# A two-block transformer kernel: the FFN's gate and up products by five Strassen groups, its second product by one

## The reference

```python
def swiglu(h, w_gate, w_up, w_down):            # D_MODEL 1024, D_FF 2816 = 22 chunks of 128
    return (jax.nn.silu(h @ w_gate) * (h @ w_up)) @ w_down

x = x + rms_norm(m, g_post_mix)                 # m: attention @ w_o
h = rms_norm(x, g_pre_ffn)
x = x + rms_norm(swiglu(h, w_gate, w_up, w_down), g_post_ffn)
```

## Time and profile before

| | before |
|---|---|
| median of 3 runs | 1280.83 us |
| profiled execution, its own time | 1281.71 us |
| its span | 1279.6 us |
| PE busy | 1270.1 us, 99% |
| DVE busy | 761.4 us, 60% |
| ACT busy | 594.1 us, 46% |
| DMA, moved | 181.01 MB |

### The profile page before, as it was taken

How to read it: one execution, slowest core, us unless ns; L and a number is a source line. 1 busy time by engine, 2 the same in 40 slices (tenths; PEclk the granted TensorE clock), 3 DMA queues, 4 the chain that set the end, 5 groups by cost and what they waited for, 6 DMA issues and landing times.

```text
span 1279.6 us, 16976 instructions
## 1 busy us (share of the span) xinstructions
PE 1270.1 (99%) x6329; PEld 1061.1 (83%) x6329; DVE 761.4 (60%) x1554; ACT 594.1 (46%) x1239; POOL 49.9 (4%) x97
## 2 busy tenths in 40 slices
PE   9999999999999999999999999999999999999998
PEld 8887777898888888888888888788878788999987
DVE  4366776654555455547675678675545534976664
ACT  5366676543453345335453324563335542463533
POOL 1010100100000000000100010000000000000000
PEclk9999999999999999999999999999999999999999
DMA  6279894222252236232525898212221022353531
GB/s 249 99 214 257 241 263 141 70 99 99 99 198 99 99 122 222 85 132 99 171 94 173 243 273 238 77 67 99 99 99 67 33 99 100 125 195 125 197 133 66
DMA packets 31937, 181.01 MB, mean 141 GB/s; under 512 B 3944, under 2 KB 4204, under 8 KB 12784
## 3 DMA queue, kind: packets, MB, share of 16 engines
q1 hardware_dynamic: 24360, 141.19, 31.6%
q0 software_dynamic: 4608, 33.56, 10.3%
q10 hardware_dynamic: 2888, 5.18, 1.2%
HBM read 171.52 MB, written 37.76 MB: 164 GB/s over the span
## 4 chain that ended last, share of the span: by engine, by line
PE 95%; DVE 1%; DMA 1%; issue 1%; POOL 0%; ACT 0%; ACTq 0%; POOLq 0%; SPq 0%; DVEq 0%
PE bank L2068 26%; PE bank L2070 26%; PE bank L2069 26%; PE sc L2244 3%; PE tp L2253 2%; PE ob L2268 1%; PE ob L2310 1%; PE sc L2070 1%; PE sc L2069 1%; PE sc L2068 1%; DMA act_hi<-act_hi 1%; PE bank L2185 1%; PE bank L2175 1%; PE bank L2194 1%; PE bank L2277 1%
## 5 line engine op out<-in xcount | busy, mean ns | idle before, releaser
L2068 PE MATMUL bank<-xT_hi,w_hi 128*128 128x512 f32 (+1 forms) x1040 | 407.5, 392 | 0.1
L2070 PE MATMUL bank<-xT_hi,w_lo 128*128 128x512 f32 (+1 forms) x1040 | 396.0, 381 | 0.0
L2069 PE MATMUL bank<-xT_lo,w_hi 128*128 128x512 f32 (+1 forms) x1040 | 395.6, 380 | 0.0
L1280 DVE TENSOR_TENSOR w_lo<-w_raw,w_hi 128x512 fp32r<-128x512 f32 x467 | 296.7, 686 | 165.5 <-ACT w_hi L723 163.9
L723 ACT ACTIVATE w_hi<-w_raw 128x512 fp32r<-128x512 f32 x467 | 261.3, 621 | 119.9 <-PE bank L2070 96.0
L2068 PEld LDWEIGHTS bank<-xT_hi,w_hi 128*128 128x128 f32 x1040 | 196.0, 188 | 39.5 <-issue 4.5
L2070 PEld LDWEIGHTS bank<-xT_hi,w_lo 128*128 128x128 f32 x1040 | 195.9, 188 | 38.0
L2069 PEld LDWEIGHTS bank<-xT_lo,w_hi 128*128 128x128 f32 x1040 | 196.3, 189 | 34.8 <-issue 1.2
L731 ACT ACTIVATE arena<-bank 128x512 f32<-128x512 f32 x74 | 43.8, 597 | 137.8 <-PE bank L2070 132.7
L2068 PE MATMUL bank<-w_hi,act_hi 128*128 128x512 f32 (+1 forms) x264 | 102.7, 389 | 0.0
L2070 PE MATMUL bank<-w_hi,act_lo 128*128 128x512 f32 (+1 forms) x264 | 101.1, 383 | 0.0
(11 more groups left out here) (287 smaller groups left out, 1742.2 us busy)
## 6 DMA issues: line engine op xcount, KB each, us to landing
w_raw<-in_weights SPq DMA_DIRECT2D x99, 1024.0 KB, 4.9
sum_dram<-in_weights POOLq DMA_DIRECT2D x24, 1024.0 KB, 9.5
w_raw<-sum_dram SPq DMA_DIRECT2D x16, 1024.0 KB, 4.8
sum_dram<-sum_dram POOLq DMA_DIRECT2D x8, 1024.0 KB, 8.5
arena<-in_bias ACTq DMA_DIRECT2D x16, 256.0 KB, 5.5
act_lo<-act_lo SPq DMA_DIRECT2D x24, 128.0 KB, 8.0
x_sb<-in_x SPq DMA_DIRECT2D x4, 512.0 KB, 6.3
w_raw<-in_weights SPq DMA_DIRECT2D x4, 512.0 KB, 8.0
```

Source lines behind the costliest of these rows:

```text
L1280: nc.vector.tensor_tensor(w_lo[SPLIT_AT[b]][:, cols], w_raw[SLOT[b]][:, cols], w_hi[SPLIT_AT[b]][:, cols].bitcast(F32), ALU.subtract).then ...
L2068: nc.tensor.matmul(ps, hi_l, hi_r, start=first, stop=False, skip_group_check=onto)
L2069: nc.tensor.matmul(ps, hi_l, lo_r, start=False, stop=False, skip_group_check=onto)
L2070: return nc.tensor.matmul(ps, lo_l, hi_r, start=False, stop=last, skip_group_check=onto)
```

## The change

The FFN is rebuilt, in four parts.

1. **Gate and up.** Two chunks stay plain. The other 20 are five Strassen groups `up0` to `up4` of four chunks, in the form of the gate groups: a product is 48 matmuls of 256 columns. Of the seven products, five are written into or added up in the bank pair X, which isn't cleared between them: ACT copies its state out after product 0, 3 and 5, and DVE adds its state to a kept copy after product 2 (from pair V), 4 (X) and 6 (pair Z).
2. **The second matrix.** One Strassen group over all 22 chunks: seven products of 11 chunks each, every one in three blocks of 4, 4 and 3 chunks, 512 columns moving. The hidden activations stay in the arena, and their left-hand sums are made in place piece by piece between the splits.
3. **Sums from DRAM.** There are ten groups to sum (5 `up`, 3 `down`, 2 gates) in place of four. They run as two chains side by side (even and odd groups), and `SUM_STEPS` says how many steps of both chains POOL takes after the memset of each head: none for heads 0 to 3, two for each of heads 4 to 15.
4. **Splits.** In the FFN a block is rounded and split in two parts of 1024 columns (1024 and 512 for a block of three chunks), not in four of 512.

The diff, cut to its core:

```diff
+SUM_STEPS = [0] * 4 + [2] * 12
+COLUMN_X = ("x11", "t1", "x21", "t2", "t3", "t4", "x22")
+COLUMN_BANK = (X, Z, V, X, X, X, Z)
+ROW_BANK = (X, V, Z, Z, X, X, X)
+DOWN_CHUNKS = ((0, 4), (4, 8), (8, HALF_FC))
...
             def sums_of_weights(g):
...
+                if k:
+                    pool.wait_ge(chain, 16 * 6 * k)
+                begin(s1, a1, chain)
                 yield
+                pool.wait_ge(chain, 16 * (6 * k + 1))
+                add(s1, a2, chain)
                 yield
+                if k:
+                    pool.wait_ge(pair_, 16 * 2 * k)
+                begin(pair_sum, p1, pair_)
+                pool.wait_ge(chain, 16 * (6 * k + 2))
+                begin(s2, sum_dram[s1, :, :], chain)
                 yield
...
+            weight_sums = [every_second(range(i, len(GROUPS), 2)) for i in range(2)]
+            def add_weights(steps):
+                step_between(weight_sums[0], steps, weight_sums[1])
             for h in range(HEADS):
-                if h >= HEADS - 6 * QUADS:
-                    step(weight_sums, 1)
                 pool.wait_ge(bias_loaded[h % 4], 16 * (h // 4 + 1))
                 nc.gpsimd.memset(biases[h % 4][0:CHUNK, BIAS_W - CHUNK:BIAS_W], NEG).then_inc(bias_ready, 1)
+                add_weights(SUM_STEPS[h])
...
 # ACT, group q
+                up_out(q, 0, kept(p1))
+                split(up + 2)
...
+                up_out(q, 1, kept(p5))
+                split(up + 3)
...
+                split(up + 4)
+                up_out(q, 3, kept(u2))
+                split(up + 5)
...
+                split(up + 6)
...
+                up_out(q, 5, lambda h: up_chunks(q, h, 0), ACT.Silu, -1.0)
...
 # DVE, group q
+                split(up + 4)
+                up_add(q, 2, p1, 0, 0)
...
+                split(up + 5)
...
+                split(up + 6)
+                up_add(q, 4, p5, 2, 2)
...
+                gated_quad(q, 0, None, p1)
+                split(up + 7)
+                split(up + 8)
+                up_add(q, 6, u2, 4, 4)
...
 # DVE, second matrix, block n
+                if n == 18:
+                    down_add(5, p5, 2)
+                if n:
+                    split(FIRST["down"] + n + 1)
...
+                if j < PRODUCTS - 1:
+                    split_left(j + 1, b)
+                for name, piece in MAKE_AT.get(n, ()):
+                    make_left(name, piece)
...
 # PE
+            def up_bank_ready(q, i, h):
...
+                if COLUMN_X[i] == "t3":
+                    pe.wait_ge(up_copied, 8 * q + 4 + h + 1)
+                if COLUMN_X[i] == "t4":
+                    pe.wait_ge(up_added, 6 * q + 2 + h + 1)
...
+            for j in range(PRODUCTS):
+                opens, order = ROW_BANK[j] not in ROW_BANK[:j], DOWN_LAST if j == PRODUCTS - 1 else DOWN_ORDER
+                for b, r in order:
...
+                    if b == 0:
+                        down_bank_ready(j, r)
```

More of the change, by code:

```diff
@@ L124, in plan @@
         add(f"wo{h}", 2, TT)
[L125 to L136, removed]
+    add("gu", PLAIN, 2 * PLAIN)
+    for q in range(UP_QUADS):
+        first[f"up{q}"] = n
+        done += [("up_full", 2 * (PRODUCTS * q + i + 1)) for i in range(PRODUCTS)]
+        n += PRODUCTS
+    first["down"] = n
+    for j in range(PRODUCTS):
+        order = DOWN_LAST if j == PRODUCTS - 1 else DOWN_ORDER
+        done += [("down_full", 2 * N_DOWN * j + order.index((b, 1)) + 1) for b in range(N_DOWN)]
+        n += N_DOWN
+    add("a_v", 2, TT)
     add("cwf", 1, TT)
@@ L168, in places @@
 def places():
[L172 to L195, removed]
-        else:
-            loaded(b, ordinary % RING)
-            ordinary += 1
-            b += 1
+    slot, loads, at, summed, blocks, count = {}, {}, {}, {}, 0, [0] * RING
@@ new lines, in places @@
+    strassen = {}
+    for g, name in enumerate(GROUPS):
+        if name.startswith("down"):
+            for j, part in enumerate(ROW_OPERANDS):
+                strassen[FIRST["down"] + N_DOWN * j + g - GROUPS.index("down0")] = g, part
+        else:
+            for i, part in enumerate(COLUMN_OPERANDS):
+                strassen[FIRST[name] + i] = g, part
+    for b in range(N_OPERANDS):
+        if b in strassen:
+            g, part = strassen[b]
+            if (g, "11") not in at:
+                for other in ROW_PARTS if GROUPS[g].startswith("down") else COLUMN_PARTS:
+                    at[g, other] = blocks
+                    blocks += 1
+            if part in SUMS:
+                summed[b] = len(SUMS) * g + SUMS.index(part)
+            else:
+                at[b] = at[g, part]
+        else:
+            at[b] = blocks
+            blocks += 1
+        slot[b] = b % RING
+        count[slot[b]] += 1
+        loads[b] = count[slot[b]]
@@ L333, in build @@
+        left_hi, left_lo = ([part[:, 0:6, :].rearrange("p c (x s) -> p (c x) s", s=ST) for part in parts]
+                            for parts in ((act_hi, xT_hi), (act_lo, xT_lo)))
+        square_junk = act_f32[:, 0, 10:12, :].rearrange("p c s -> p (c s)")
+        m21 = view(7168, 2, S)
         av = view(0, TT, W)
@@ L1272, in split_parts @@
                     return
[L1273 removed]
+                for i, cols in enumerate(columns_of(b)):
                     if (b, i) == (0, 1):
@@ new lines, in up_add, with gated_quad @@
+            def up_add(q, i, dst, copied, done):
+                for h in range(2):
+                    dve.wait_ge(up_copied, 8 * q + copied + h + 1)
+                    dve.wait_ge(up_full, 2 * (PRODUCTS * q + i) + h + 1)
+                    nc.vector.tensor_tensor(dst[:, h, :], dst[:, h, :], up_bank[COLUMN_BANK[i]][h][:, :], ALU.add).then_inc(up_added, 1)
+            def gated_quad(q, tok, silu, other):
+                for h in range(2):
+                    c = PLAIN + KW * q + 2 * h
+                    place = hidden[:, c:c + 2, ST * tok:ST * tok + ST]
+                    ins = nc.vector.tensor_tensor(place, place if silu is None else silu[:, h, :].rearrange("p (m s) -> p m s", s=ST),
+                                                  other[:, h, :].rearrange("p (m s) -> p m s", s=ST), ALU.mult)
+                ins.then_inc(hidden_done, 1)
@@ new lines, in _, with gain_c21 @@
+            split_xT("pre2", 1)
+            for t in range(2, TT):
+                begin_variance("post2", t)
+                gain_down(t, 1, p5[:, t - 2, :], p5[:, t - 2, :], True)
+            def gain_c21(t):
+                gain_down(t, 0, m21[:, t - 2, :], down_bank[X][t - 2][:, :], False).then_inc(c21_free, 1)
+            parts = split_parts(FIRST["a_v"] + 1)
+            gain_c21(2)
+            variance("post2", 2, D)
+            step(parts, 1)
+            update(2)
+            gain_c21(3)
```

963 lines of the change are left out of this document (490 added, 473 removed).

## The result

The kernel after takes 1448.57 us (median of four runs, 1444.78 to 1452.84). The kernel before, run on the same chip beside it, takes 1280.69 us. The ratio is 1.131, with an interval of 1.127 to 1.134: **slower by 13%**, where 1462 us was predicted and 1395 to 1510 given as the range. The profiled execution took 1452.84 us, the longest of the four, 171.1 us more than that of before; the medians are 167.9 us apart.

A forecast was written before the change was run, and what follows sets the result against it. PE was taken as the bound, busy 99% of the span. 1281.7 - 20.4 + 151 + 1.7 + 4 + 22.5 + 8.5 + 3 + 9 + 2 = 1463.0, less 0.9 for the median: 1462 us, range 1395 to 1510.

The forecast's parts named there:

- Theory A: Whole kernel: sums delay the attention's heads and the FFN stalls, giving 1462 us, own range 1430 to 1495; chance 0.68.
- Matmuls, -20.4: FFN on PE: gate and up fall from 217.6 to 201.3 us, second matrix from 108.8 to 104.7; together -20.4 us.
- Sums in the attention, memset of head 15 at 360: Attention, POOL: 56 DMAs of 4.15 us plus 40 of other traffic precede head 15's memset, at 360 us; +151 us.
- rival B: Attention: sums cheaper side by side, 3.0 us per transfer, +87 in place of +151, 1394 us; 0.13 with the 1361 variant.
- C's bare latency: Attention: each round costs its pair's landing, 8.2 or 14.3 us; head 15 at 397, +188, total 1499 us; chance 0.13.
- Clock and POOL's last steps, +5.7: Attention's end: half clock when PE resumes, +1.7 us; two more POOL steps before the first norm's roots, +4.
- Group stalls, 5 x 4.5: FFN's five groups: PE waits before product 5 for DVE's addition behind a split, 4.5 us each, +22.5 us.
- Clock, 5 x 1.7: FFN's five groups: half clock behind each idle before product 5 costs 1.7 us more each, +8.5 us.
- Forms t3 and t4, +3: FFN, group `up0`: DVE makes these forms between its splits, so product 4 comes late; +3 us (0 to 8).
- Second matrix, +9: FFN's second matrix: DVE's work at blocks 15 to 18 delays product 6, plus clock and smaller waits; +9 us (0 to 20).
- Before `a_v`, +2: Before `a_v`: the norm's chain is hidden by PE work as before, but DVE comes late; +2 us (-1 to 8).

## Why the prediction was right

Theory A held in its mechanism and nearly in its sizes. That the total came so close is in part luck: the attention's terms came to 156.7 us and 141.7 were measured, the FFN's to 24.6 and 29.7 were measured, and the two errors partly cancel. Of POOL's memsets, heads 7 to 15 are 23.6 us apart in the mean, as forecast, but the gaps go from 15.6 to 29.9 us.

- **Matmuls, -20.4.** The pitches are those of the earlier trace rows: a product of a group in step takes 48 x 0.1198. Of the 20.4 us, 8 reach the time in the kernel without sums; the step holds, but I had most of the small waits that eat it under other names.
- **Sums in the attention, memset of head 15 at 360.** It came at 347.70. A DMA took 3.99 us, not 4.15 (9 us less over 56), and the other traffic (queues q1 and q10) 14.5% of the 261 us from 87 to 348, 38, not 40. Counted from PE's place at 210.2 this is 348.7 - 210.2 = +138.5 in place of +151. The 4.15 may have held some waiting, a part of what rival B said, which isn't shown; B's 3.0 is the price of a copy alone (3.04), and the accumulations at 4.94 keep the mean at 4. C's bare latency is near for one chain and wrong for two. Two readings of rows were off without harm: the share of 1.02 belongs to 159 to 169 us, at 339 GB/s, while the earlier trace rows show 169 to 179 at 1.00 and 224 GB/s, so 1.02 at far less than the loads' rate was not what the trace shows; and the 4.5 us for the landing of head 4's bias block stand in no row, it took 6.3, while in after its memset stands at 87.36, near the 88 used.
- **Clock and POOL's last steps, +5.7.** With the root at +141.7, 3.2 are left for both. The clock cost more than I counted, since the mean from 90 to 385 us was 0.77, but I take it that beneath a wait for POOL this costs nothing; the last steps were nearly hidden.
- **Group stalls, 5 x 4.5.** 4.34 in four groups, 5.24 in the first, 22.6 us in all against 22.5. The unseen durations came out as chosen: 1.0 on ACT and 1.2 on DVE for 1024 columns. **Clock, 5 x 1.7**: 10.7 us in all, 1.3 to 2.7 each. I took the loss behind one idle of 1.98 us for the loss behind any; behind four idles of the same 4.34 us it was 2.5, 2.7, 1.3 and 2.0.
- **Forms t3 and t4, +3**: two waits of 0.67 and 0.76. **Second matrix, +9**: 3.48 at the place named, 2.5 for the clock, 0.74 at another, 6.7. **Before `a_v`, +2**: waits of 1.59 and 1.53 and 1.4 for the clock, 4.5.

The FFN's terms as measured make -20.4 + 22.6 + 10.7 + 1.4 + 6.7 + 4.5 = +25.5; the marks say +29.7. From one stall's end to the next (502.95 to 550.37) a group takes 47.42 us, and 7 x 5.75 + 4.34 + 2.5 is 47.1: 0.3 us a group, 1.5 in all. That and 2.7 us elsewhere I can't place; the kernel without sums has about 3 us of the same kind.

What the prediction doesn't tell is the way out. No placing of the 64 DMAs that ran was free: the FFN has 58 loads of its own, about 3 us each, and with 32 DMAs of sums beside them it gives back 37 us. No version that ran with the sums beats the kernel before, and the one without any is 0.7% below it.

What stays open: whether sums of weights made on an engine, or three buffers for `w_raw`, would keep the 8 us, and so whether the FFN's 37 us are late landings or a want of capacity. Neither was tried.

## What to carry to other kernels

A step that waits for a DMA in the program of an engine that others need delays them by the longer of two prices: the landing (about 8 us for a step of one chain here), or the engines' time of all that is in flight (3.0 us for a copied and 4.9 for an accumulated MB). Set it against the period of what is queued behind it: 9 us to a head took one step and not two. Before saving 20 us of PE with operands summed by DMA, add up the DMA engines' time of the sums and of the loads beside them: here some 256 us of it for the 64 sums that save these 20. Where PE waits for an addition that stands behind a split begun by the same event, try to swap the two: one moved line was worth 30 us.

## What the runs showed of the hardware

- Two chains in flight gain nothing once the engines are full (share 1.01 over 295 us): 3.04 us of all engines for a copied MB, 4.94 for an accumulated one, and landings of 11.8 us in the median for the 48 DMAs from `in_weights`.
- A load that lands in 4.9 us in the median where no sums run took 12.8 beside them. The queues share the engines, and nothing in these rows shows the urgent load preferred.
- The clock: an idle of 1.98 us cost 1.7 us behind it, four of 4.34 us cost 1.3 to 2.7 each, and in 753 to 757 us all 4 us ran at 0.50 after an idle of 3.48. In the attention, with ten idles of up to 17 us, the mean was 0.77.
